# A two-layer hybrid mixer on one core: orders of the engines' queues changed in seven places

## What is computed

```python
h = rms_norm(x, norm_gain) * (1 + scale) + shift          # scale, shift, gate = silu(cond) @ w_ada + b_ada
z = h @ w_in                                              # 1024 -> 3840, split into the inputs of four branches
y_a = b_gate * conv3(c_gate * u)                          # A: short gated convolution
y_b = softmax(rope(norm(q)) @ rope(norm(k)).T) @ v        # B: grouped-query attention, 4 heads, 64 wide
y_c = rms_norm(retention_fwd(q, k, v) + retention_bwd)    # C: retention in chunks of 128
y_d = rms_norm((softmax(q1 k1) - lam * softmax(q2 k2)) @ v) * gain     # D: differential attention, 4 heads
merged = sum(sigmoid(h @ w_mgate[i]) * ((y_i * silu(gate_i)) @ w_branch[i]) for i in "ABCD")
x = x + gate * (merged @ w_out)
```

## Time and profile before

| | us |
|---|---|
| runs | 1431.5, 1430.44, 1427.73 |
| median | 1430.44 |
| profiled execution | 1431.54 |
| its span | 1429.3 |
| PE busy | 1366.3 |
| DVE busy | 864.7 |
| ACT busy | 570.4 |
| POOL busy | 77.5 |

### The profile page before, as it was taken

The page is one execution under the profiler, slowest core; times in us unless marked ns, Lnnn a source line. Parts: engine busy times, 40 slices in busy tenths (PEclk is TensorE's granted clock), DMA queues, the critical chain, the costliest instruction groups (busy, mean ns, idle before and its releaser), DMA issues.

```text
span 1429.3 us, 27105 instructions
## 1 busy us (share of the span) xinstructions
PE 1366.3 (96%) x10357; PEld 1320.5 (92%) x10357; DVE 864.7 (60%) x1764; ACT 570.4 (40%) x1252; POOL 77.5 (5%) x102
## 2 busy tenths in 40 slices
PE   5899999999999999999999999999999999999998
PEld 2799889999989999999999988999998999999998
DVE  2566676556555598777565467754755567654355
ACT  2566555334453222213343555542445422222242
POOL 0100000010000000100010000001100000001000
PEclk9999999999999999999999999999999999999999
DMA  9412212123012342465232211112221134213322
GB/s 320 151 59 64 75 38 67 33 72 111 30 30 93 126 137 70 130 175 176 71 119 79 88 43 57 55 60 74 75 67 31 34 120 143 75 50 106 121 72 75
DMA packets 106308, 127.71 MB, mean 89 GB/s; under 512 B 4076, under 2 KB 92744, under 8 KB 106184
## 3 DMA queue, kind: packets, MB, share of 16 engines
q1 hardware_dynamic: 101560, 110.76, 24.2%
q0 software_dynamic: 4624, 15.22, 3.6%
HBM read 119.66 MB, written 6.31 MB: 88 GB/s over the span
## 4 chain that ended last, share of the span: by engine, by line
PE 78%; DVE 11%; issue 5%; ACT 4%; POOL 1%; DMA 0%; DVEq 0%; SPq 0%; ACTq 0%; POOLq 0%
PE G L1437 37%; PE G L1435 19%; PE BK L1451 8%; PE TO L1532 3%; PE TP L1519 3%; PE TP L1493 2%; PE S L1510 1%; DVE w_lo L1086 1%; DVE neg_max L1258 1%; POOL rs L753 1%; PE BK L1462 1%; PE S L1513 1%; PE S L1512 1%; DVE h_lo L1362 1%; ACT w_hi L876 1%
## 5 line engine op out<-in xcount | busy, mean ns | idle before, releaser
L1086 DVE TENSOR_TENSOR w_lo<-w_raw,w_hi 128x512 fp32r<-128x512 f32 x312 | 208.2, 688 | 116.5 <-ACT w_hi L876 115.3
L1437 PE MATMUL G<-h_lo,w_hi 128*128 128x320 f32 x1472 | 248.9, 311 | 0.0
L1437 PE MATMUL G<-h_hi,w_lo 128*128 128x320 f32 x1472 | 248.7, 311 | 0.0
L1437 PE MATMUL G<-h_hi,w_hi 128*128 128x320 f32 x1472 | 248.1, 311 | 0.0
L1437 PEld LDWEIGHTS G<-h_lo,w_hi 128*128 128x128 f32 x1472 | 223.0, 188 | 0.5
L1437 PEld LDWEIGHTS G<-h_hi,w_lo 128*128 128x128 f32 x1472 | 223.1, 188 | 0.2
L1437 PEld LDWEIGHTS G<-h_hi,w_hi 128*128 128x128 f32 x1472 | 222.0, 188 | 0.8 <-issue 0.3
L876 ACT ACTIVATE w_hi<-w_raw 128x512 fp32r<-128x512 f32 x312 | 184.9, 623 | 18.9 <-DMA w_raw<-in_w_branch 13.7
L963 ACT ACTIVATE tg<-G 128x320 f32<-128x320 f32 x128 | 55.7, 435 | 237.4 <-PE G L1437 236.0
L1435 PE MATMUL G<-w_hi,h_hi 128*128 128x256 f32 x960 | 138.3, 287 | 5.0 <-DVE ra L1371 3.2
L999 ACT ACTIVATE work<-S,neg_max 128x640 f32<-128x640 f32 (+1 forms) x120 | 85.1, 710 | 144.2 <-DVE neg_max L1258 129.8
(11 more groups left out here) (226 smaller groups left out, 1589.9 us busy)
## 6 DMA issues: line engine op xcount, KB each, us to landing
w_raw<-in_w_mgate SPq DMA_DIRECT2D x32, 1024.0 KB, 5.4
w_raw<-in_w_in SPq DMA_DIRECT2D x30, 1024.0 KB, 5.5
w_raw<-in_w_ada SPq DMA_DIRECT2D x17, 1024.0 KB, 5.3
w_raw<-in_w_branch SPq DMA_DIRECT2D x32, 256.0 KB, 5.8
w_raw<-in_w_out SPq DMA_DIRECT2D x8, 1024.0 KB, 4.9
early_raw<-in_w_ada SPq DMA_DIRECT2D x6, 1024.0 KB, 11.8
work<-in_x_sample POOLq DMA_DIRECT2D x4, 512.0 KB, 6.0
work<-gate_rows POOLq DMA_DIRECT2D x4, 512.0 KB, 5.0
```

Of the source, the lines that this page charges most:

```text
L1086: V.tensor_tensor(w_lo[:, s.n % 2, a:b, :], raw_rows(s), w_hi[:, s.n % 2, a:b, :].bitcast(F32), ALU.subtract).then_inc(lo_done, 1)
L1437: ins = mm(g[:, 0:HALF], a[:, w, kt, c], b[:, kt, half], start=first, stop=last)
```

## The change

Seven edits, all to the order in which things are done; the arithmetic is the same.

1. The queries of branch B are turned in the bank TO instead of TP (D's stay in TP); `cat` of branch B then also waits for TO's transposes.
2. `onorm` of branch D goes from priority 7 to 11, so behind `map` (9) and `comb` (10) of its group.
3. The low part of a weight piece becomes a step of its own, `lowpart`, one pass after the rounding (in the same pass in the first pair of projections of a stage). In the start two low parts stand before the last chunk of w_ada and two after the last quarter; the roundings move from the seventh to the eighth chunk.
4. `ysplit` and `convend` are made in two halves, and a `branch` waits for the half it reads.
5. `msplit` of tiles 3 and 4 comes after the first and second output unit. The squares of an output come one unit later (except in the last quarter) and into `gflat`. The turns of one of the folded w_ada sums (the last of layer 0) come at passes 17 and 19 instead of 8 and 9.
6. The second tile of layer 0 is turned early (`hearly`, before the fifth chunk of w_ada) and into S; x tile 2 is loaded by POOL after all eight chunks instead of after six.
7. The key groups of branch D are spread over the projections from the fourth plan element on instead of the ninth.

```diff
-                rows.append((e + 3, 7, [Step("onorm", l=l, br=br, t=t, part=0)]))
-                rows.append((e + 5, 7, [Step("onorm", l=l, br=br, t=t, part=1)]))
+                rows.append((e + 3, 11, [Step("onorm", l=l, br=br, t=t, part=0)]))
+                rows.append((e + 5, 11, [Step("onorm", l=l, br=br, t=t, part=1)]))
...
-                    body += quarter(i // 2 - 1) + pieces(p1[0][0]) * (i == 6)
-                body += [Step("ada", l=0, c=c, of=early[i])] + [Step("xfirst", l=0, t=2)] * (i == 5)
-            body += [Step("xfirst", l=0, t=3), Step("xfirst", l=0, t=4), *quarter(3), Step("hturn", l=0, t=1), ...
+                    body += quarter(i // 2 - 1)
+                if i == 7:
+                    first = pieces(p1[0][0])
+                    body += first + [Step("lowpart", of=first[p]) for p in (0, 1)]
+                body += [Step("hearly", l=0, t=1)] * (i == 4)
+                body += [Step("ada", l=0, c=c, of=early[i])]
+            body += [Step("xfirst", l=0, t=t) for t in (2, 3, 4)] + [*quarter(3), Step("lowpart", of=first[2]),
+                     Step("lowpart", of=first[3]), Step("hturn", l=0, t=1), ...
...
-        body += flat(u[:8]) + spread(u[8:], key_groups(l, "D"))
+        body += flat(u[:3]) + spread(u[3:], key_groups(l, "D"))
...
-        m[bg + 11] = m[bg + 11] + [Step("convend", l=l, b=0), Step("convend", l=l, b=1), Step("ysplit", l=l, br="A")]
+        m[bg + 11] = m[bg + 11] + [Step("convend", l=l, b=b, half=h) for h in range(2) for b in range(2)] + ysplits("A")
...
-        body += flat(u) + [Step("msplit", l=l, t=t) for t in range(2, NT)]
+        body += flat(u) + [Step("msplit", l=l, t=2)]
         u = units(p9)
+        outs = [u[3 * i + 2][0] for i in range(4 * NT)]
+        for i, s in enumerate(outs):
+            at = 3 * (i + (s.q < 3)) + 2
+            u[at] = u[at] + [Step("square", l=l, t=s.t, q=s.q, of=s)]
+        for t in (3, 4):
+            u[3 * (t - 3) + 2] = u[3 * (t - 3) + 2] + [Step("msplit", l=l, t=t)]
...
-                due += [(passes + delay + 8 + i, Step("adas", l=l, c=a, half=i)) for i in range(2 * kh)]
+                due += [(passes + delay + (8 + i if len(later) != 4 else 17 + 2 * i), Step("adas", l=l, c=a, half=i)) for i in range(2 * kh)]
...
-                due += [(passes + delay + gap * i, p) for i, p in enumerate(pieces(nxt[c.n]))]
+                for i, piece in enumerate(pieces(nxt[c.n])):
+                    due += [(passes + delay + gap * i, piece), (passes + delay + gap * i + 1 * (delay > 1), Step("lowpart", of=piece))]
...
+                elif k == "turn" and s.br == "B" and s.what == "q":                       # ACT
+                    act.wait_ge(to_done, s.to + 1)
+                    act.wait_ge(sc_done, s.q_free)
+                    nc.scalar.activation(q_stack[:, s.qs % 2, :, :], TO[:, :].rearrange("p (m n) -> p m n", m=4), ACT.Copy).then_inc(to_evac, 1)
...
-                    nc.scalar.activation(y_hi[:, :, :], y_source(s.br), ACT.Copy).then_inc(yh_done, 1)
+                    half = slice(s.half * HALF, (s.half + 1) * HALF)
+                    nc.scalar.activation(y_hi[:, :, half], y_source(s.br)[:, :, half], ACT.Copy).then_inc(yh_done, 1)
...
-                    pe.wait_ge(yl_done, s.before["ysplit"])
+                    pe.wait_ge(yl_done, s.before["ysplit"] - 1 + s.half)
...
+                elif k == "hearly":                                                       # PE
+                    pe.wait_ge(xs_done, s.t + 1)
+                    for kt in range(KT):
+                        ins = nc.tensor.transpose(S[:, kt * P:(kt + 1) * P], x_scaled(0, s.t)[:, kt * P:(kt + 1) * P], ident)
+                    ins.then_inc(tp_done, 1)
+                elif k == "turn" and s.br == "B" and s.what == "q":
+                    pe.wait_ge(to_evac, s.to)
+                    pe.wait_ge(cat_lo, s.cat)
+                    for i in range(4):
+                        ins = nc.tensor.transpose(TO[:, i * P:(i + 1) * P], catb[:, i * P:(i + 1) * P], ident)
+                    ins.then_inc(to_done, 1)
```

More of the change, by code:

```diff
@@ L164, in make_plan, with ysplits @@
         phases = []
+        def ysplits(br):
+            return [Step("ysplit", l=l, br=br, half=h) for h in range(2)]
         def tok(src, col, dest):
@@ L275, in make_plan @@
         u = units(p6)
-        u[0] = u[0] + [Step("ysplit", l=l, br="B")]
+        u[0] = u[0] + ysplits("B")
         body += flat(u[:45])
@@ L407, in number @@
                 n["mod"] = n["tg"]
-        if k in ("turn", "pt", "hturn", "rturn"):
+        if k in ("turn", "pt", "hturn", "rturn") and not (k == "turn" and s.br == "B" and s.what == "q"):
             s.tp = n["tp"]
@@ L413, in number @@
             n["hturn"] += 1
-        if k in ("pv", "oturn", "yturn", "delta", "rout", "adat"):
+        if k in ("pv", "oturn", "yturn", "delta", "rout", "adat") or (k == "turn" and s.br == "B" and s.what == "q"):
             s.to = n["to"]
@@ L464, in number @@
                  and m.part == (s.h // 2 if s.br == "D" else 0)][0]
-            s.qs, s.q_need = q.qs, q.tp + 1
+            s.qs, s.q_need = q.qs, (q.to if s.br == "B" else q.tp) + 1
             qslot_sc[s.qs] = n["sc"]
+            s.k_need = max(k.tp + 1 for k in plan if k.kind == "turn" and k.what == "k" and (k.l, k.br) == (s.l, s.br))
         if k in ("hstat", "onorm", "ystat", "vec"):
@@ L882, in _ @@
                         nc.scalar.activation(squares, x_res[s.t], ACT.Square, accum_out=ssum[:, s.t:s.t + 1]).then_inc(sq_done, 1)
[L883 to L887, removed]
+                elif k == "square":
+                    act.wait_ge(x_added, s.of.before["out"] + 1)
+                    act.wait_ge(yl_done, s.before["ysplit"])
+                    act.wait_ge(sq_done, NT + s.of.before["out"])
+                    nc.scalar.activation(gflat[:, 0:CW], x_res[s.t][:, s.q * CW:(s.q + 1) * CW], ACT.Square,
                                          accum_out=qsum[:, s.t, s.q:s.q + 1]).then_inc(sq_done, 1)
@@ L912, in _ @@
                     c = 0 if s.t == 0 else 1
+                    turned = S if (s.l, s.t) == (0, 1) else TP
                     for kt in range(4):
-                        ins = nc.scalar.activation(hf[s.t % 2][:, kt * P:(kt + 1) * P], TP[:, kt * P:(kt + 1) * P], ACT.Identity,
+                        ins = nc.scalar.activation(hf[s.t % 2][:, kt * P:(kt + 1) * P], turned[:, kt * P:(kt + 1) * P], ACT.Identity,
                                                    scale=gs[:, kt, c:c + 1], bias=mod[:, s.l, kt, c:c + 1])
@@ L1012, in _ @@
                     if s.br == "A":
-                        act.wait_ge(y_ready, 2 * (s.l + 1))
+                        act.wait_ge(y_ready, 4 * s.l + 2 * s.half + 2)
                     else:
@@ L1212, in _ @@
                     dve.wait_ge(big_evac, s.before["big_act"])
-                    V.tensor_tensor(merged[:, 2 + s.b, :], merged[:, 2 + s.b, :], merged[:, s.b, :], ALU.mult).then_inc(y_ready, 1)
+                    half = slice(s.half * HALF, (s.half + 1) * HALF)
+                    V.tensor_tensor(merged[:, 2 + s.b, half], merged[:, 2 + s.b, half], merged[:, s.b, half], ALU.mult).then_inc(y_ready, 1)
                 elif k == "ysplit":
                     dve.wait_ge(yh_done, s.before["ysplit"] + 1)
-                    V.tensor_tensor(y_lo[:, :, :], y_source(s.br), y_hi[:, :, :].bitcast(F32), ALU.subtract).then_inc(yl_done, 1)
+                    half = slice(s.half * HALF, (s.half + 1) * HALF)
+                    V.tensor_tensor(y_lo[:, :, half], y_source(s.br)[:, :, half], y_hi[:, :, half].bitcast(F32), ALU.subtract).then_inc(yl_done, 1)
                 elif k == "vec":
@@ L1481, in _ @@
                     ins.then_inc(as_done, 1)
-                elif k == "hturn":
+                elif k == "hearly":
[3 more added lines that the diff above has]
+                    ins.then_inc(tp_done, 1)
+                elif k == "hturn" and (s.l, s.t) != (0, 1):
                     tp_free(s)
@@ L1501, in _ @@
                         pe.wait_ge(as_evac, s.before["adas"])
-                    pe.wait_ge(tp_evac, s.q_need)
+                    pe.wait_ge(to_evac if s.br == "B" else tp_evac, s.q_need)
+                    if s.br == "B" and s.t == 0 and s.h == 0:
+                        pe.wait_ge(tp_evac, s.k_need)
                     for i, comp in enumerate(s.comps):
```

19 lines of the change are left out of this document (13 added, 6 removed).

## The result

The changed kernel takes **1407.81 us** (median; 1407.01 to 1408.66), the kernel before 1430.24: a ratio of 0.9844, 95% interval 0.9832 to 0.9856, 22.4 us less. The forecast was 1409. The profiled execution has a span of 1406.7 us, against 1429.3.

What follows compares the result with a forecast made beforehand. PE was taken as the bound, busy 1366.3 of 1429.3 us. Gains of 6.9, 5.6, 4.2, 4.9, 0.9 and 0.3 less 1.2 made 21.6: 1409.9, forecast as 1409 us; own range 1404 to 1415, 8 in 10 for 1401 to 1422.

Steps and rivals of the forecast that it cites:

- Query turn of B: Branch B: turning queries in TO removes PE's waits for ACT's copy to q_stack; 6.9 us gained, bounds 5.9 to 8.4.
- rival (a): Removed waits come back at the next link of the ACT and DVE chains; 1417 us if half returns, chance 0.18.
- Norms: Branch D: maxima ahead of norms on DVE shorten PE's score-matmul waits; 5.6 us gained, bounds 3 to 7.
- Low parts: Weight low parts a pass later: no separate gain; 1.2 us cost at three chunk starts sharing the ring, bounds 0 to 9.
- The wait for tg at chunk starts: Sign against the forecast: the branch matmul waiting for tg at chunk starts would prove it wrong.
- rival (c): Low parts come too late at 62 chunk starts, making the kernel slower; 1437 us and above, chance 0.07.
- y in halves: Branch outputs split in halves shorten PE's waits for y_lo in four places; 4.2 us gained, bounds 3 to 4.6.
- Merged in steps: Start of w_out: later splits of tiles 3 and 4 remove PE's waits and a clock fall; 4.9 us, bounds 3.2 to 5.
- Start: Second tile turned early and fewer low parts ahead of PE's copy; 0.9 us gained, bounds -0.5 to 2.6.
- Keys of D: Key stage, layer 0: first wait stays near 2.1 us, small ones behind it go; 0.3 us gained, bounds -0.5 to 3.8.
- The dip near 97 still there: Sign: the granted clock still falls near 97 us, in the key stage of layer 0; that fall is priced at 1.7 us.
- rival (b): More goes than taken: key stage keeps its clock and loses its wait, other S waits go; 1403 us, chance 0.11.

Runs made afterwards that it cites:

- experiment 3: The kernel before with only the low parts moved one pass behind their rounding (the first chunk's stay); 1431.72 us, ratio 1.0011.
- e1_ring: The changed kernel with low parts back in their rounding's pass while a half of w_ada shares the raw-buffer ring; 1398.35 us, ratio 0.9782.
- f1_btp: e1_ring with the query turn of branch B in TP again; 1406.65 us.
- g2_start: e1_ring with the start as before: second tile turned behind the last fold and in TP, first low parts where they were; 1402.81 us.
- experiment 4: Parts of the change undone one at a time on e1_ring; 1401.57 to 1406.65 us.
- e4_lag_alone: The run of experiment 3: the kernel before with only the later low parts; 1431.72 us.
- f4_keys8: e1_ring with the keys of branch D spread from the eighth unit again; 1401.57 us.
- e2_nolag: The changed kernel with every low part back in the pass of its rounding, in all stages; 1402.23 us.
- g4_nolag_norms: The changed kernel with every low part in its rounding's pass and the norms of branch D ahead of the maxima; 1409.27 us.
- f3_msteps: e1_ring with all merged tiles split before the first output and the w_ada additions' turn at its old pass; 1401.81 us.
- e3_norms: The changed kernel with the norms of branch D ahead of the maxima again; 1412.45 us.

## Why the prediction was right, and where it was not

**Query turn of B: right.** 6.9 predicted, 7.0 aligned (8.3 timed). Each tile gives 0.9 to 1.0, and one a layer 0.7; at the first tile of B a wait of 0.8 us for DVE's combination took its place (L1562 <- L1297, 2.5 us in 4 against 1.0 in 2 before), and that is the only link of branch B at which rival (a) showed.

**Norms: right in size, wrong in attribution.** 5.6 against 5.2 to 5.9. But the score waits fell by 7.7 us, not 5.6. The step that failed is "DVE gains only where something urgent is queued behind: that is in the 5.6 above, and I count nothing twice". The six waits "behind other things" did not stay: with the low parts alone later, six of the twelve went (8.3 to 4.5, experiment 3). In the trace before, a low part stands shortly in front of the maximum at ten of the twelve waits, also at two of the three that I gave to the norm alone: at the first of them (152.67) DVE had stood 1.47 us for ACT before the low part, and the norm came only then:

```profile
149.29 0.69 DVE L1086 TENSOR_TENSOR w_lo<-w_raw,w_hi 128x512 fp32r<-128x512 f32 x1 [1.47 <-ACT w_hi L876]
```

**Low parts: wrong twice.** Off the ring they gained 3 to 4 us where I counted nothing. On the ring they cost 8.9 to 9.5 where I charged 1.2, at the very end of my bound of 9 and beyond it. The failed step is the slip: I priced "one pass later" as 3.1 us by the instructions between two low parts in the last branch stage, and took the three chunk starts as alike. At 581.50 a norm of branch C that waits for POOL lies in the same pass, and the last low part slipped by 6.5 us (587.37; aligned, it stood at 580.91). I also left out a second effect: the weights, issued later, come directly ahead of a half of w_ada, and with GpSimd's load beside it that half took 16.6 us against 5.1. At the long wait DVE, and not ACT's tanh, is then what stands in front of PE; at the second one, 0.91 us, it is the tanh, as I had it. The wait for tg at chunk starts was on my list of what would prove me wrong, and it is there; what rival (c) had was the mechanism, at two chunk starts (three in experiment 3) instead of 62.

**y in halves: right in mechanism, a little small.** 4.2 predicted; 4.4 aligned in the change, 5.2 to 5.5 undone, above my bound of 4.6. Grouping would not have paid: the Trainium skill (Perfetto Trace Analysis, Optimizing Scalar/DVE Operations) advises fewer, larger instructions only where the engine is the limit. Here it is not, and the trace agrees: y_lo in halves costs DVE 1.56 us in two (591.44) instead of 1.49 in one, and PE gained at once.

**Merged in steps: right in mechanism, too large.** 4.9 predicted, with a bound of 3.2 below. Aligned from before to after, w_out gives 4.0 net (2.5 and 1.5), and 0.9 of it, in layer 1, experiment 3 has from the later low parts alone. Undone on the faster version the part is worth 2.3 to 3.5, because there the wait is 1.7 us and no clock falls. One wait of 0.8 us stays (674.40), which I had at nothing: an h_lo that itself waits 1.12 us for ACT is still ahead of the evacuation. In `e1_ring` it is gone.

**Start: right, with luck of the clock on top.** 0.9 predicted (bounds -0.5 to 2.6), 2.0 aligned in the change and 2.4 in the undo, the rest of the 4.5 being the clock in the key stage and chance. The wait of 3.27 at 38.03 fell to 0.64, as foreseen (0.65), and the eight transposes do cost their time in the chain of folds (24.76). The first projection came at 41.04 against 42.7, because in this execution PE had the full clock for some 3 us of the chain: the fold at 22.52 took 1.16 us, in the kernel before 1.94.

```profile
22.52 1.16 PE L1492 MATMUL BK<-merged,cond_w 128*32 128x256 f32 x16
...
24.76 1.91 PE L1515 MATMUL S<-cst,za 128*128 128x128 f32 x8
```

In `f1_btp`, which has the new start, every fold ran slow, as in the kernel before, and its first projection is where I had put it:

```profile
42.52 2.08 PE L1462 MATMUL G<-w_hi,h_hi 128*128 128x256 f32 x8 [1.66 <-ACT h_hi L921]
```

Compared like with like, the start is worth 0.6 us (before against `f1_btp`, at the twelfth pass) to 1.2 (`g2_start` against the changed kernel, both with the full clock once near 20 us). In `e1_ring` the folds ran at full clock for longer, and there PE waited for the transfers of w_ada instead:

```profile
PE BK L1493 <- DMA early_raw<-in_w_ada: 4.8, 3, 2.3
```

**Keys of D: right on the wait, wrong on the clock.** The wait stayed at 2.1, as predicted. "The dip near 97 still there" failed, and with it 1.7 us: of rival (b), "the key stage keeps its clock and loses its wait", the first half came, and by chance as far as the runs show. The small waits behind, which I had at 0.3, were 1.8 over both layers.

So the 21.6 predicted became 22.6 aligned (22.4 timed) like this, in us against my terms, the parts as undone in experiment 4 and the start as it is in the change: start +1.1, keys of D +3.3, low parts off the ring +2.9, y +1.0, B +0.1, norms -0.4, merged -2.6, together +5.4; 3.3 more that no single undo brings back, most of it in D and at w_out, where the later low parts and another part each give what the other would; and 7.7 of ring cost that I had too small. That the total came out is luck: errors of some 8 us on either side cancel. Experiment 3 shows the same on a smaller scale, where a small net is the sum of +5.9 and of gains of nearly the same size.

Some of the prediction's own sums are off, none of them in the forecast: 1417 with the ring cost at its bound is 1425, not 1423; 0.45 us in each of 62 chunks is 28 us, more than the gain of 21.6, and 1.3 us in each would be 81 us, not 54; and the upper bounds of the gains lead to 1400, not 1397.

## What to carry to other kernels

When a step is moved "by one pass", price the pass in which it lands, not one like it somewhere else: list what is queued between the old and the new place at each of its occurrences, waits for other engines included, and then follow the buffer that it frees to the load behind it and to the transfer that this load will overtake or delay. A relaxation of order pays where a buffer is free and costs where a ring is shared, so make it conditional on the stage: here that was worth 9 us. And undo each part on its own before believing a total.

## What the runs showed of the hardware

**The clock after a short wait is not determined by the wait.** Of the executions in which PE idled 2.1 us for the first keys of D after more than 10 full us at 2.4 GHz, those of `after`, `e1_ring`, `e4_lag_alone` and six more kept the clock, those of `before`, `f4_keys8` and `g2_start` lost it (1.2 GHz, granted 0.5, in windows of 2.7 to 3.5 us right behind). `e2_nolag` and `g4_nolag_norms`, which are the same program up to there, idled 2.72 and 2.73: the one kept it, the other lost it.

```profile
90.01 1.06 PE L1534 MATMUL TP<-cst,work 128*128 128x128 f32 x8 [2.72 <-DVE work L1280]
```
```profile
90.00:94.00 4.00, 3.99 (x30) 4.00 (x31) 3.93 (x11) 2.12 (x4) 0.00 (x0) 1.00 0.56 168
```
```profile
88.34 1.37 PE L1534 MATMUL TP<-cst,work 128*128 128x128 f32 x8 [2.73 <-DVE work L1280]
```
```profile
89.80:92.40 2.60, 2.60 (x11) 2.60 (x11) 2.53 (x8) 2.07 (x4) 0.00 (x0) 0.50 0.88 270
```

From full clock, waits of 1.7 us (w_out in `f3_msteps`, the second tile of layer 1) never cost it in these traces; those of 2.06 (y_lo) and 2.86 (w_out) in `e4_lag_alone`, 2.3 (w_out before), 3.1 and 3.6 did. Between 1.7 and 3.1 us (2.72 in `e2_nolag` did not, 2.73 in `g4_nolag_norms` did) a forecast should carry the 1.4 to 1.8 us that the fall costs with a chance, and not as a fact either way. What decides between the two is open.

**A load of 1 MB took between 5 and 17 us, by what was ahead of it and beside it.** Issued 1.3 us behind 1.25 MB on the same queue it took 7.4 to 7.7 us (`after`, `e3_norms`, `e4_lag_alone`, the half at 563 to 575), and 14.0 to 16.6 when 512 KB of GpSimd's queue followed 3.4 us later. Issued 7.4 us behind, with the same 512 KB, it took 5.0 to 5.3 us in eight kernels and 8.7 to 11.4 in three; what makes the difference among these is open.
